# Two halves of a split weight interleaved in SBUF, and a start offset for each matmul operand

## What is computed

```python
for i in range(DEPTH):                                   # first block; gqa at i=0, diff attention at i=1
    hx = hx + 0.5 * mx[:, 2] * _swiglu(_pre(hx, norm_w[i, 0], ...), w_gate[i, 0], w_up[i, 0], w_down[i, 0])
    hx = hx + mx[:, 5] * mixer(_pre(hx, norm_w[i, 1], ...), w_in, w_out)
    hx = hx + 0.5 * mx[:, 8] * _swiglu(_pre(hx, norm_w[i, 2], ...), w_gate[i, 1], w_up[i, 1], w_down[i, 1])
    ...                                                  # the same for the context hc, as long as it is needed
for l in range(DEPTH):                                   # second block; retention + dilated at 0, gla at 1
    x = x + 0.5 * _swiglu_2(_rmsnorm_2(x, g1), w_gate, w_up, w_down)
    x = x + mixer(_rmsnorm_2(x, g2), w_in, w_out)
    x = x + 0.5 * _swiglu_2(_rmsnorm_2(x, g3), w_gate, w_up, w_down)
```

## Time and profile before

| | us |
|---|---|
| median of 3 runs | 2853.32 (2852.08 to 2854.17) |
| the profiled execution | 2851.07 |
| its span, first to last instruction | 2849.3 |
| PE busy | 2770.8 |
| DVE busy | 1770.9 |
| ACT busy | 1204.0 |
| granted TensorE clock, mean | 0.992 of full speed |

### The profile page before, as it was taken

One profiled execution on the slowest core, in us unless ns is written; L12 is line 12 of the kernel. 1 busy time (PEld: TensorE's weight loads), 2 busy tenths in 40 slices (PEclk: granted clock), 3 DMA queues, 4 the chain that ended last, 5 costly groups with the idle time before them and its releaser, 6 DMA issues.

```text
span 2849.3 us, 45845 instructions
## 1 busy us (share of the span) xinstructions
PE 2770.8 (97%) x17468; PEld 2439.7 (86%) x17468; DVE 1770.9 (62%) x2690; ACT 1204.0 (42%) x1808; POOL 200.2 (7%) x246
## 2 busy tenths in 40 slices
PE   7999999999999999999998999999989999999998
PEld 5888876678888788888876999999879999998998
DVE  5977244847874287732538655667666666667665
ACT  4222223833222243222326555654445555544553
POOL 0100011010100100001100101001000000000001
PEclk9999999999999999999999999999989999999999
DMA  8666222025663346533330556656425666653554
GB/s 305 208 197 184 91 87 89 1 74 177 207 191 117 113 155 192 176 96 97 98 99 19 166 182 187 183 176 212 120 88 177 181 186 186 183 169 98 173 177 137
DMA packets 118688, 424.31 MB, mean 149 GB/s; under 512 B 13280, under 2 KB 14321, under 8 KB 117409
## 3 DMA queue, kind: packets, MB, share of 16 engines
q1 hardware_dynamic: 98528, 353.41, 40.4%
q0 software_dynamic: 18992, 68.09, 8.1%
q10 hardware_dynamic: 1040, 1.05, 0.1%
HBM read 421.45 MB, written 1.05 MB: 148 GB/s over the span
## 4 chain that ended last, share of the span: by engine, by line
PE 88%; DVE 7%; ACT 2%; issue 2%; DMA 1%; SPq 0%; DVEq 0%; ACTq 0%
PE bank L721 28%; PE bank L723 28%; PE bank L722 28%; DVE WL L1559 1%; ACT WH L1222 1%; DMA f_nat<-in_ada_n 1%; DVE rstd L1755 1%; DVE g_max L1857 1%; DVE d_small L1919 1%; PE bank L854 1%; PE bank L962 0%; PE bank L939 0%; DVE g_p L1877 0%; DVE tn L1765 0%; DVE d_p L1928 0%
## 5 line engine op out<-in xcount | busy, mean ns | idle before, releaser
L721 PE MATMUL bank<-XH,WH 128*128 128x256 f32 (+1 forms) x3776 | 1227.1, 325 | 21.6 <-DVE XL L1774 6.2
L722 PE MATMUL bank<-XL,WH 128*128 128x256 f32 (+1 forms) x3776 | 1215.1, 322 | 0.0
L723 PE MATMUL bank<-XH,WL 128*128 128x256 f32 (+1 forms) x3776 | 1214.9, 322 | 0.0
L1559 DVE TENSOR_TENSOR WL<-raw,WH 128x1024 fp32r<-128x1024 f32 (+1 forms) x664 | 806.1, 1218 | 643.3 <-ACT WH L1222 640.1
L1222 ACT ACTIVATE WH<-raw 128x1024 fp32r<-128x1024 f32 (+1 forms) x664 | 681.9, 1034 | 817.4 <-PE bank L723 805.1
L721 PEld LDWEIGHTS bank<-XH,WH 128*128 128x128 f32 x3776 | 723.1, 192 | 83.8 <-issue 11.8
L722 PEld LDWEIGHTS bank<-XL,WH 128*128 128x128 f32 x3776 | 723.5, 192 | 55.1 <-issue 3.1
L723 PEld LDWEIGHTS bank<-XH,WL 128*128 128x128 f32 x3776 | 723.0, 191 | 52.3
L721 PE MATMUL bank<-HH,WH 128*128 128x256 f32 (+1 forms) x1408 | 451.0, 320 | 0.0
L722 PE MATMUL bank<-HL,WH 128*128 128x256 f32 (+1 forms) x1408 | 450.9, 320 | 0.0
L723 PE MATMUL bank<-HH,WL 128*128 128x256 f32 (+1 forms) x1408 | 450.9, 320 | 0.0
(11 more groups left out here) (318 smaller groups left out, 1617.4 us busy)
## 6 DMA issues: line engine op xcount, KB each, us to landing
a_rows<-in_ada_t POOLq DMA_DIRECT2D x124, 512.0 KB, 4.2
raw<-in_ffn_w_gate SPq DMA_DIRECT2D x88, 512.0 KB, 3.6
raw<-in_ffn_w_up SPq DMA_DIRECT2D x88, 512.0 KB, 4.3
raw<-in_ffn_w_down SPq DMA_DIRECT2D x64, 512.0 KB, 3.6
raw<-in_ffn_pre_w_gate SPq DMA_DIRECT2D x44, 512.0 KB, 3.6
raw<-in_ffn_pre_w_up SPq DMA_DIRECT2D x44, 512.0 KB, 4.3
raw<-in_ffn_post_w_gate SPq DMA_DIRECT2D x44, 512.0 KB, 3.6
raw<-in_ffn_post_w_up SPq DMA_DIRECT2D x44, 512.0 KB, 4.3
```

The source lines that it names most:

```text
L721: nc.tensor.matmul(o, WH[:, j % 4, k, :], high, start=start, stop=False)
L722: nc.tensor.matmul(o, WH[:, j % 4, k, :], low, start=False, stop=False)
L723: return nc.tensor.matmul(o, WL[:, j % 4, k, :], high, start=False, stop=stop)
L1559: nc.vector.tensor_tensor(WL[:, b, 0:d, :], raw[:, b, 0:d, :], WH[:, b, 0:d, :].bitcast(F32), ALU.subtract).then_inc(split_done, 1)
```

## The change

`WH` and `WL` become two views of one tensor, `w_pair`, whose last dimension of two holds high and low side by side. So a stationary tile of 128 columns is read with a step of two words over 1 KB, and the k index moves it by 1 KB; ACT writes its copy and DVE reads and writes with a step of two. `XH`, `XL` become views of `x_all`, `HH`, `HL` of `h_all`, each with 128 words of padding, and each stage's view begins at an offset of its own, in words: `NORM_X` for the 13 norms' outputs, `MIX_X` for the four mixers' outputs, `FFN_H` for the hidden values of the eight feed-forwards. `skew` grows from 32 to 48 words. A norm of 256 columns writes to columns from 256 in every case (`c0`). No instruction is added or taken away, nor a wait.

```diff
-        XH = sb("XH", [P, DT, 2 * S], F32R)
-        XL = sb("XL", [P, DT, 2 * S], F32R)
+        X_PAD, H_PAD = 128, 128
+        x_all = sb("x_all", [P, 2 * DT * 2 * S + X_PAD], F32R)
         raw = sb("raw", [P, 4, DT, P])
-        WH = sb("WH", [P, 4, DT, P], F32R)
-        WL = sb("WL", [P, 4, DT, P], F32R)
+        w_pair = sb("w_pair", [P, 4, DT, P, 2], F32R)
+        WH, WL = w_pair[:, :, :, :, 0], w_pair[:, :, :, :, 1]
...
-        skew = sb("skew", [P, 32])
+        skew = sb("skew", [P, 48])
+
+        def x_view(at, low):
+
+            at += DT * 2 * S if low else 0
+            return x_all[:, at:at + DT * 2 * S].rearrange("p (k n) -> p k n", k=DT)
+
+        NORM_X = (0, 16, 32, 48, 8, 16, 32, 48, 48, 8, 24, 24, 0)
+        MIX_X = (24, 0, 48, 24)
+        FFN_H = (16, 32, 48, 0, 16, 32, 48, 8)
...
-        HH, HL = arena(("HH", [P, FT, 2 * S], F32R), ("HL", [P, FT, 2 * S], F32R))
+        (h_all,) = arena(("h_all", [P, 2 * FT * 2 * S + H_PAD], F32R))
+
+        def h_view(at, low):
+
+            at += FT * 2 * S if low else 0
+            return h_all[:, at:at + FT * 2 * S].rearrange("p (k n) -> p k n", k=FT)
...
+            n["x"] = NORM_X[n["i"]]
+            n["c0"] = S if t == S else 0
...
-                            last = nc.scalar.activation(XH[:, k, cs], tn[:, k % 2, cs], ACTF.Identity, bias=n["shift"](k, half))
+                            last = nc.scalar.activation(x_high(n["x"])[:, k, n["c0"] + half * S:n["c0"] + half * S + S], tn[:, k % 2, cs], ACTF.Identity, bias=n["shift"](k, half))
```

More of the change, by code:

```diff
@@ L393, in mixer @@
             steps.append(("mix", m))
-            out_proj(w_out, t, mix_ready[m], gate)
+            out_proj(w_out, t, m, gate)
         GQA_SIDE = {(1, 1): [("rope", 0), ("v", 0)], (1, 2): [("v", 1)], (1, 3): [("swap", 0), ("swap", 1)],
@@ L1102, in gla_low @@
                 for k in range(DT):
-                    nc.tensor.matmul(bank[4][:, 0:S], a_wh[:, k, :], XH[:, k, S:2 * S], start=(k == 0), stop=False)
-                    nc.tensor.matmul(bank[4][:, 0:S], a_wh[:, k, :], XL[:, k, S:2 * S], start=False, stop=False)
-                    last = nc.tensor.matmul(bank[4][:, 0:S], a_wl[:, k, :], XH[:, k, S:2 * S], start=False, stop=(k == DT - 1))
+                    nc.tensor.matmul(bank[4][:, 0:S], a_wh[:, k, :], x_high(MIX_X[3])[:, k, S:2 * S], start=(k == 0), stop=False)
+                    nc.tensor.matmul(bank[4][:, 0:S], a_wh[:, k, :], x_low(MIX_X[3])[:, k, S:2 * S], start=False, stop=False)
+                    last = nc.tensor.matmul(bank[4][:, 0:S], a_wl[:, k, :], x_high(MIX_X[3])[:, k, S:2 * S], start=False, stop=(k == DT - 1))
                 last.then_inc(gs["low"], 1)
@@ L1711, in scaled_low @@
                 dve.wait_ge(n_high, n["h0"] + k + 1)
-                nc.vector.scalar_tensor_tensor(out=XL[:, k, S:2 * S], in0=xT[:, k, 0:S], scalar=n["weight"](k, 0),
-                                               in1=XH[:, k, S:2 * S].bitcast(F32), op0=ALU.mult, op1=ALU.subtract).then_inc(n_low, 1)
+                nc.vector.scalar_tensor_tensor(out=x_low(n["x"])[:, k, S:2 * S], in0=xT[:, k, 0:S], scalar=n["weight"](k, 0),
+                                               in1=x_high(n["x"])[:, k, S:2 * S].bitcast(F32), op0=ALU.mult, op1=ALU.subtract).then_inc(n_low, 1)
             def restate(d):
@@ L1773, in rest @@
                             cs = slice(half * S, half * S + S)
+                            xs = slice(n["c0"] + half * S, n["c0"] + half * S + S)
                             last = nc.vector.scalar_tensor_tensor(
-                                out=XL[:, k, cs], in0=tn[:, k % 2, cs], scalar=n["shift"](k, half),
-                                in1=XH[:, k, cs].bitcast(F32), op0=ALU.add, op1=ALU.subtract)
+                                out=x_low(n["x"])[:, k, xs], in0=tn[:, k % 2, cs], scalar=n["shift"](k, half),
+                                in1=x_high(n["x"])[:, k, xs].bitcast(F32), op0=ALU.add, op1=ALU.subtract)
                     else:
-                        last = nc.vector.tensor_tensor(XL[:, k, 0:t], tn[:, k % 2, 0:t], XH[:, k, 0:t].bitcast(F32), ALU.subtract)
+                        last = nc.vector.tensor_tensor(x_low(n["x"])[:, k, 0:t], tn[:, k % 2, 0:t], x_high(n["x"])[:, k, 0:t].bitcast(F32), ALU.subtract)
                     last.then_inc(n_low, 1)
```

61 lines of the change are left out of this document (32 added, 29 removed).

## The result

The changed kernel takes 2897.98 us (median of 4 runs, 2895.82 to 2899.70), the one before 2853.25 beside it: a ratio of 1.0157, with a 95% interval from 1.0139 to 1.0174. It is slower by 44.7 us, where 2782.5 was predicted. The profiled execution took 2897.7, with a span of 2895.9.

A forecast was written before the change was run, and what follows sets the result against it. PE was taken to bound the kernel, by matmul count times step. 16.0 + 1.9 + 26.9 + 10.2 + 21.1 - 3.5 - 1.8 = 70.8 us less gave 2782.5; range of 8 in 10: 2695 to 2960.

The forecast's parts named there:

- the rival of a slow split: ACT's and DVE's split writes each take twice their time and hold PE back: some 105 us, to 2958; chance 0.09.
- The reading of X against H: PE steps at 256 columns: 120.0 ns with X, 113.3 with H, the difference put down to place against the weights.
- The rule of the Trainium skill: PE has two read ports of its own, so by this rule alone no operand's place would matter.
- units of 64 bytes: Steps exceed the columns' time by one to three times 6.7 ns, the time in which 64 moving-row bytes pass.
- the rival in which the extra goes altogether: All split matmuls step at 106.7 ns at 256 and 213.3 at 512 columns: 180 us less, 2673; chance 0.17.
- the lockstep: At a step of two, weight load and moving operand both pass 1 KB in the same time, keeping their distance.
- The bound from below: Limit for steps with the load at a step of two: all extra goes, down to 106.7 and 213.3 ns.
- the 26.9 and 10.2 us of X at 256: Gains forecast for X at 256 columns: 4032 matmuls by a full unit, 3072 at 8 or 24 words by half.
- Slower: the load reads twice the places: The extra doubles on all split matmuls, to 3054, or one unit more each, to 2957; chance 0.20, harsh form 0.05.
- Offsets alone: Offsets shift steps as today, the step of two does nothing: 13.9 us less, to 2839; chance 0.10.

The follow-up runs named there:

- the map: Kernel before, every split matmul loading stationary tiles from a zeroed tensor nobody writes, load step and distance set by stage and piece; 2986.41 us in one run.
- the fastest one: Against the kernel before: contiguous weights, 512-column stages at distance 0, X at 256 64 bytes ahead of three weight buffers, level with the fourth; 2815.12 us, ratio 0.9866.

## Why the prediction was wrong

**Right: what counts.** Some 39 of the 46.6 us are in the step from start to start; no wait for the split came up, and DVE's work with a step of two cost nothing. ACT's copy did cost 90 ns each, which had been put at nothing; its cover held, as PE's idle time behind the split shows (5.5 against 5.2 us), so the rival of a slow split falls.

**Right: the step depends on the operands' distance.** The reading of X against H in the earlier trace rows and `a_wh` in the earlier trace rows holds at a step of one: the kernel with 64 bytes ahead of the weights changed steps of X without moving X. The rule of the Trainium skill that was weighed in the prediction (SBUF — State Buffer, "A bandwidth-pool intuition that's wrong") thus fails here too, by up to 6.7 ns a matmul. The reading as units of 64 bytes was too neat: the map has 4, 8 and 16 bytes at 118 to 120, at 512 columns 8 bytes cost as much as 192 (233.3), and one distance can run at 113.3 or at 117.8. And the 6.7 ns of H at 256 over the columns' 106.7 were hardly a matter of place: the load alone takes 111.7. So the rival in which the extra goes altogether, to 106.7, lay below what a load at a step of one allows.

**Wrong: the lockstep.** The step that failed is "a stage whose offset is a multiple of 64 bytes other than 0 comes one unit below today's X step, 113.3 and 220.0". The bound from below was argued from the two operands' relative motion, and the load was held to be free, since it "touches places no faster than the moving operand". The runs showed a price of the load itself: 117.8 against 111.7 ns with nothing else to wait for, and at 256 columns no distance that averaged below 118.3. This rules out 113.3, and with it the 26.9 and 10.2 us of X at 256; and it makes H at 256, whose 113.3 were to be kept in three stages, lose 6.6 to 7.7 ns in all five. In lockstep the distance did stop being a source of gain rather than become one: 119.9 to 121.2 at 256 columns. At 512 columns, where the load has time to spare, the step still went from 226.7 to 233.3 at distance 0; there the offsets gave back 3.4 ns at best (230.0 at 48 words), not 13.3. A load at a step of one pays for distance, one at a step of two pays at every distance tried.

The 2898 measured lies in the range of 8 in 10, 2695 to 2960, only because that range was wide enough to hold the slower rivals; the forecast's own range of 2747 to 2818 doesn't hold it, and the direction was wrong.

The Trainium skill has a rule nearer to this than the one I weighed (Advanced Engine Details and Errata, "Memory Cachelines"): SBUF is read in lines of 16 bytes, and at least two accesses must fall into one line, or there is a penalty. Here four words of a contiguous tile share such a line, two at a step of two, one or two at three, one at four. The trace agrees about the large jump (118, then 173 and 233 ns), and disagrees that a step of two is free: it costs 6.1 ns on a load and, in ACT's copy, 90 ns in 1034.

**The rivals.** "Slower: the load reads twice the places" named the operand and the direction, and its milder form, a unit on each matmul, the size of a unit. It came true for X at 512 and H at 256: 6672 matmuls, 39 to 44 us, and not for all 15,552 (104 us). The kinds that had a unit more already didn't get another. Weight loads above 192 ns were named as its sign, and they came, at 193 to 199; the steps of 127 or more named beside them did not. "Offsets alone" was mis-sized: 8 us slower instead of 13.9 faster, because H at 256 lost more (11.0 of steps) and of X at 256 only norm 5's up gained its full unit among the up stages, and X gained 17 us instead of 37.1 in all. At 512 columns it was right in direction and size for X (17.0 lost, 17.9 by the rival).

**Open.** Why the distance acts at all, and what throws a stage from the beat of 113.3 to that of 117.8: the map tells what helps, not the mechanism. It isn't shown either whether the unit that X at 512 gained under a step of two is the load's own 6 ns or a collision; a load there has 227 ns for what takes 118, which speaks for the latter, but this is argued only. The 7.6 us of the changed kernel outside the steps are absent in the run at all offsets 0, whose granted clock stood at 0.50 for 44.2 us, less than the 47.0 of the kernel before; that fits the clock as their cause and doesn't prove it. Of the two beats the record shows one thing more: H at 256, 64 bytes short of the weights in four kernels, held 113.4 in all five stages in the two where the stage ahead had pieces at distance 0 (the kernel before and the fastest one), and fell to 117.8 in three or four of five in the two where it had none. The map has a case against a simple rule: its pieces at 448 bytes, behind pieces at 256, ran at 117.8.

## What to carry to other kernels

Keep stationary tiles contiguous: interleave two weights tile by tile, not element by element, since a load at a step of two costs 6 ns, and at three or four 60 to 120 ns, on every matmul that its pace can reach; with 512 moving columns, where it can't, the step of two still cost 6.6 ns at distance 0. Where a kernel is bound by equal matmuls one behind another, the start of the moving operand against the stationary one is worth up to 6.7 ns each, and choosing it per stage at a step of one, with every fourth piece at distance 0, took 1.3% off this kernel. Before arguing how a new access pattern will behave, measure its floor with a narrow moving operand, and map the patterns piece by piece from a tensor that nobody writes: one run gave all of them.

## What was not expected of the hardware

- The granted clock fell to 0.50 when whole stages had moving operands of 64 and 128 columns, though PE was busy throughout (461 matmuls in 100 us). With one piece in four cut to 64 columns it stayed at 1.00 in norm 5's up, with the load at a step of one, and fell at times in norm 11's up, with the load at a step of three:

```profile
1590.00:1700.00 110.00, 110.00 (x937) 110.00 (x936) 65.41 (x83) 65.20 (x89) 0.00 (x0) 1.00 0.62 191
2700.00:2860.00 160.00, 157.47 (x1024) 157.13 (x1023) 81.00 (x111) 73.86 (x100) 0.72 (x1) 0.84 0.48 144
```

- A load at a step of four takes 233.3 ns a matmul at either clock level, a load at a step of three 173 at full clock and 213.3, as step one, at the low one.
- The same code at the same places has two stable beats, 113.3 and 117.8 ns, and a stage whose every fourth piece had distance 0 ran the other three mostly at the faster.
